# A one-core MoE backbone: the experts' down weights move from the SyncE DMA queue to the ScalarE DMA queue

## What is computed

```python
def moe_ffn(h, router_w, router_bias, w_gate, w_up, w_down, sh_gate, sh_up, sh_down):
    scores = jax.nn.sigmoid(h.astype(jnp.float32) @ router_w.astype(jnp.float32))
    _, idx = lax.top_k(scores + router_bias.astype(jnp.float32), TOP_K)      # 8 of 64 experts
    ...
    def expert_block(args):
        tok, e = args
        xb = h_pad[tok]
        hid = jax.nn.silu(xb @ w_gate[e]) * (xb @ w_up[e])                   # 1024 -> 256
        return hid @ w_down[e]                                               # 256 -> 1024
    ...
```

## Time and profile before

| | us |
|---|---|
| time, median of 3 runs | 2188.66 (2185.78 to 2189.01) |
| the profiled execution, its own time | 2187.06 |
| its span, first to last instruction | 2185.2 |
| PE busy in the span | 1723.6 (79%) |
| ACT busy in the span | 321.0 (15%) |

### The profile page before, as it was taken

How to read it: one execution, slowest core, us unless ns; L and a number is a source line. 1 busy time by engine, 2 the same in 40 slices (tenths; PEclk the granted TensorE clock), 3 DMA queues, 4 the chain that set the end, 5 groups by cost and what they waited for, 6 DMA issues and landing times. The chain is left out here.

```text
span 2185.2 us, 23250 instructions
## 1 busy us (share of the span) xinstructions
PE 1723.6 (79%) x8645; PEld 784.1 (36%) x8645; DVE 590.6 (27%) x1343; ACT 321.0 (15%) x698; POOL 252.3 (12%) x235
## 2 busy tenths in 40 slices
PE   4999999985999899989966997876967657547740
PEld 2544444452443333333323444442422212212210
DVE  2213445252222122222116426431211111101106
ACT  2002333020111111111101105310100000000000
POOL 0301222000111111111100002101111100100002
PEclk8999999997999999999987998887988878778975
DMA  9325662044699999999948140062789999999944
GB/s 339 109 77 184 215 232 102 0 185 183 231 419 421 412 402 386 416 415 397 415 178 342 77 154 5 0 240 95 270 331 382 367 388 367 365 375 371 387 159 173
DMA packets 130368, 577.27 MB, mean 264 GB/s; under 512 B 20146, under 2 KB 25665, under 8 KB 79824
## 3 DMA queue, kind: packets, MB, share of 16 engines
q1 hardware_dynamic: 108112, 523.75, 60.8%
q0 software_dynamic: 22144, 52.02, 6.4%
HBM read 559.91 MB, written 43.05 MB: 276 GB/s over the span
## 5 line engine op out<-in xcount | busy, mean ns | idle before, releaser
L1600 PE MATMUL ps<-wb,pool 128*32 128x512 f32 (+2 forms) x3168 | 570.1, 649 | 200.1 <-issue 198.5
L1600 PEld LDWEIGHTS ps<-wb,pool 128*32 128x32 f32 (+2 forms) x3168 | 188.6, 132 | 577.0 <-issue 577.0
L1614 DVE TENSOR_TENSOR moe_hid<-moe_sg,ps 128x256 f32<-128x256 f32 x74 | 31.1, 421 | 838.4 <-ACT moe_sg L1608 838.4
L1640 PE MATMUL ps<-hT,moe_hidT 128*32 128x512 f32 (+2 forms) x808 | 203.9, 595 | 9.9 <-DVE moe_hidT L1629 7.6
L1640 PE MATMUL ps<-pool,moe_hidT 128*32 128x512 f32 (+2 forms) x776 | 203.6, 595 | 7.7 <-DVE moe_hidT L1629 5.5
L1525 POOL DMA_INDIRECT y_rows<-moe_y,moe_index x74 | 74.2, 1003 | 1048.6 <-ACT moe_y L1656 1027.1
L2005 PE MATMUL ps<-wb,hT 128*128 128x512 f32 x320 | 140.3, 600 | 1.6 <-issue 1.6
L1608 ACT ACTIVATE moe_sg<-ps 128x256 f32<-128x256 f32 x74 | 28.4, 384 | 716.1 <-PE ps L1600 716.1
L1574 PE MATMUL ps<-const,pool 128*128 128x128 f32 x592 | 97.6, 289 | 21.3 <-DMA pool<-h_rows,moe_index 21.3
L1517 POOL DMA_INDIRECT pool<-h_rows,moe_index x74 | 75.2, 1016 | 293.9 <-DVE moe_index L1564 272.0
L1574 PEld LDWEIGHTS ps<-const,pool 128*128 128x128 f32 x592 | 80.2, 195 | 63.1 <-issue 41.6
(11 more groups left out here) (288 smaller groups left out, 1639.7 us busy)
## 6 DMA issues: line engine op xcount, KB each, us to landing
wb<-in_expert_w_gate_dram SPq DMA_DIRECT2D x128, 1024.0 KB, 10.7
wb<-in_expert_w_up_dram SPq DMA_DIRECT2D x128, 1024.0 KB, 16.1
pool<-in_expert_w_down_dram SPq DMA_DIRECT2D x64, 1024.0 KB, 15.4
hT<-in_expert_w_down_dram SPq DMA_DIRECT2D x64, 1024.0 KB, 14.5
wb<-in_ada_w_dram SPq DMA_DIRECT2D x24, 2048.0 KB, 9.6
mix_yr<-y_rows SPq DMA_DIRECT2D x8, 2048.0 KB, 10.6
wb<-in_diff_w_in_dram SPq DMA_DIRECT2D x6, 2048.0 KB, 14.8
wb<-in_ab_w_in_dram SPq DMA_DIRECT2D x4, 2048.0 KB, 16.4
```

Source lines behind the costliest of these rows:

```text
L1600: mm = nc.tensor.matmul(core.ps[lo:lo + width, n % 2, :], xT[:, n % 2, k, lo:lo + width], w[:, k], start=k == 0, stop=k == KD - 1, skip_gr ...
L1640: mm = nc.tensor.matmul(core.ps[lo:lo + width, 2 + half, :], hidT[:, n % 2, k, lo:lo + width], wd_at(q % RING, half, k), start=k == 0, sto ...
```

## The change

`sp_weights` is split. `sp_gate_up` on SP has the gate and up transfers alone, from expert 4 on. `act_down` on ACT has the down transfers: those of experts 0 to 3 ahead of ACT's first instruction of the stage, the others behind `act_y` of the round that frees their slot. Nothing else differs: the same transfers, slots, sizes and semaphores.

```diff
-        def sp_weights(sp, q):
+        def sp_gate_up(sp, q):
+            sp.wait_ge(gu_ready, plan.last(q - RING) + 1)
+            r.load_gate_up(sp, q, r.expert(sp, q))
+
+        def act_down(act, q):
+
             s = q % RING
-            e = r.plan.seq[q] if q < plan.static else r.expert(sp, q)
+            e = r.plan.seq[q] if q < plan.static else r.expert(act, q)
             if q >= RING:
-                sp.wait_ge(gu_ready, plan.last(q - RING) + 1)
-                r.load_gate_up(sp, q, e)
-                sp.wait_ge(down1_ready, plan.last(q - RING) + 1)
+                act.wait_ge(down1_ready, plan.last(q - RING) + 1)
             src = r.of(r.down_src, e)
             if s < 2:
-                sp.dma_start(wd[:, s, :], src).then_inc(d_in[s], 16)
+                act.dma_start(wd[:, s, :], src).then_inc(d_in[s], 16)
             else:
-                sp.dma_start(core.hT[:, 4 * (s - 2):4 * (s - 1), :].rearrange("p k t -> p (k t)"), src).then_inc(d_in[s], 16)
+                act.dma_start(core.hT[:, 4 * (s - 2):4 * (s - 1), :].rearrange("p k t -> p (k t)"), src).then_inc(d_in[s], 16)
...
-                for q in range(E):
-                    sp_weights(sp, q)
+                for q in range(RING, E):
+                    sp_gate_up(sp, q)
...
             def _(act):
+                for q in range(RING):
+                    act_down(act, q)
                 act_take_x(act, 0)
                 for n in range(R):
                     if n >= 1:
                         act_y(act, n - 1)
+                        for q in range(RING, E):
+                            if plan.last(q - RING) == n - 1:
+                                act_down(act, q)
                     act_silu(act, n)
```

## The result

The changed kernel takes 2212.51 us in the median of 4 runs (2209.16 to 2217.46), the kernel before 2187.91: a ratio of 1.0115, 95% interval [1.0094, 1.0136]. It is slower by 24.6 us, where I had forecast slower by 60. The sign and the range (2170 to 2265) held. Ratios leave out one execution of a later kernel (the first run of one queue), which took 2905 us at a granted clock of 0.59 where the others have about 0.9; the median given there, 2155.80, would be 2155.66 without it.

A forecast was written before the change was run, and what follows sets the result against it. Layer 1 from round 7 on was taken as bound by DMA bytes, PE waiting for gate and up weights. Terms 15.0 + 37.1 + 4.5 + 3 = 59.6 us on 2187.06 gave 2247 us, range 2170 to 2265.

The forecast's parts named there:

- Removed: SP's wait for `down1_ready` goes, so the second expert's gate issues earlier; worth nothing because the pipe was full.
- What bounds it: Layer 1 from round 7 on is a race for bytes: PE waits for gate and up weights, not downs.
- the unit: Time per 1 MB transfer with busy DMA engines in layer 1, taken as 3.0 us from three waits.
- rival 1: Service in issue order: S (gate/up products' start) at T (previous end) + 15.6; 15 us gained, 2172; 0.23 together with rival 4.
- Equal turns: SP's and ACT's queues each get half the DMA engines while both have work; 0.60 for 2220 to 2265.
- seven trios behind smaller rounds: Layer 1 waits of three-expert rounds behind one- or two-expert rounds: pipe empty 5.3 us more each, 37.1 us.
- six behind a trio: Layer 1 waits of three-expert rounds right behind another: downs take half rate from gate and up, +2.5 us each, 15.0.
- ACT's cost of zero: ACT's added number reads and down issues, 3.3 to 5.3 us, are covered before silu; cost 0.
- Rival 3: ACT blocks on its queue, issues take over 3 us and silu is late; 2287 us, chance 0.05.
- Layer 0: The pipe can't empty there; gate and up come later by about one down, once: +3 us.
- six short waits: Layer 1 waits under 3 us, for gate and up issued at T; number read behind SP's wait adds 0.75 us each, 4.5.
- The rule: Several issuing engines share the 16 DMA engines; read as time, about no change, 2187: rival 2, chance 0.10.

The follow-up runs named there:

- one-queue kernel: Against the kernel before: all transfers stay on SP's queue, issued as gate and up of all freed slots at T, then their downs; 2155.80, again 2155.19 us.
- the read ahead: Changed kernel (two queues) with the expert's number read ahead of SP's wait for the slot; 2204.23, again 2204.10 us, ratio 1.0083.
- half-size runs: Half of each down matrix fetched, in the kernel with one queue and in that with two and the number read ahead; 2077.16 and 2103.83 us.

## Why the prediction was right, and where it was wrong

| term | forecast, us | measured, us |
|---|---|---|
| SP's wait for the downs removed, new order of issue ("Removed") | 0 | -31 (2155.2 against 2186.5) |
| downs on a queue of their own | +55 (15 + 37 + 3) | +49 (2204.1 against 2155.2) |
| number read behind the wait | +4.5 | +8.8 (2212.9 against 2204.1) |
| sum | +60 | +26 in those runs, +24.6 in the first ones |

**What bounds it** was right: layer 1 from round 7 on, gate and up and not down.

**The wrong step** is in "Removed": "But the pipe was full in that time, so an earlier issue alone gives nothing." That term was put at 0 and measured -31 us. It rested on one number for the unit, 3.0 us, fitted to three waits, pauses and POOL's transfers included; with a number fitted to them the waits could only come out as full pipes. From 1600 to 2050 us the profile lists 151 issues of expert weights in the kernel before and 161 and 162 in the two runs of the one-queue kernel: 2.98 us a transfer before, 2.8 with the new order. At 2.8 us each, the 10 or 11 transfers more make about 30 us. The pause could be seen. In the trace before, this is the time to landing of the down of 32, issued at 1816.18:

```profile
L1507 SPq DMA_DIRECT2D pool<-in_expert_w_down_dram x1: 333/333/333, 1816.2 to 1816.2; - x1
...
DMA to landing us min/median/max: 4.9/4.9/4.9
```

4.9 us is what a transfer takes with nothing ahead of it (5.1). So the queue had no backlog left when SP at last issued it, and from 1816 to 1818 us the engines moved 307 GB/s, where they moved 434 in the two us before. The DMA share of 0.93 said the same, and I explained it away. With the new order a trio behind a trio has one down fewer ahead of it and no such pause. That is rival 1's gain, which I had capped at 35 us and guessed at 15; its S at T + 15.6 for round 17 measured T + 16.0 and T + 14.5 in the one-queue kernel.

**Equal turns** was right, as the landings show in pairs. The term of +55 measured +49, but its parts were not all right, and the closeness of the sum is in part luck. The seven trios behind smaller rounds were forecast at +37 and measured +40 and +41, and the reason that I gave is seen: the pipe stands empty ahead of T. The six behind a trio were forecast at +15 and measured +0.2 and +1.9. For those I had four units start at T + 3.6 and only 2.1 of them landed when the downs join; in the changed kernel three had landed 10.5 us behind T of 16 (the third at 1840.3), before the first down. The pause ahead of T may help here too, since no backlog is left in front of them (share 0.00 against 0.92 above); that was not tested by itself. Against the kernel before, where a part of the 31 us gained is mixed in, these six went -1.6 us each and the seven +4.1.

**ACT's cost of zero** held. ACT issues in 0.34 us, and the wait of silu is still one for PE's products (`L1611` after `L1603`, 745.4 us in 74 times, where it was 716.1). Rival 3 was no case.

**Layer 0** was forecast at +3; alone, with the read behind the wait, it measured +3.6 (1.0019), an interval of 1 to 7 us.

**The read** was put at six short waits, +4.5, and nothing for the thirteen long ones. It cost 8.8. The long waits start later as well: with the read ahead, the six stretches up to a trio behind a trio are 2.7 to 5.9 us shorter than in the changed kernel and the seven others 1.7 to 2.6. What layer 0 has of it was not separated.

**The rule** of the Trainium skill (DMA: Bandwidth & Descriptors, section "Issuing engines are not separate DMA queues") holds as to where the bytes go: both queues run on the same 16 engines and interleave, as the paired landings show, and two queues move no more than one (404 GB/s in layer 0, where one moved 409). Read as "a second queue changes no time" it does not hold in this kernel, where the interleaving cost 49 us of 2155.

One thing is open. The half-size runs leave some 27 us of cost on half the bytes, slightly more than half of 49. Whether a small part of the cost is due to the 0.6 us later issue behind `act_y` was not tested.

## What to carry to other kernels

A queue is also an order. When the DMA engines are the bound, put transfers that are needed later *behind* the others in the same queue; on a queue of their own they take equal turns and overtake. Before calling a pipe full, look for transfers that land in the unloaded time in the middle of it, and don't fit the unit to the waits that it is to explain. Price a change of issue order and a change of queue as two terms, since here they were -31 and +49. Read what an issue needs from a table ahead of the wait and not behind it; here that was worth 8.8 us.

## What the runs showed of the hardware

Two hardware queues with work take turns so evenly that their 1 MB transfers land within 0.8 us of one another (1846.0 and 1846.7, 1852.1 and 1852.9), one of each in 5 to 6 us, where two transfers of one queue with nothing else under way land 2.5 us apart (1815.5 and 1818.0). The two queues together move as much for each unit of busy share as one (410 and 409 GB/s). ACT issues a transfer in 0.34 us, as fast as SP (0.33 to 0.38). With three of four slots in use, what the ring fetched ahead of need is missing as work for the engines later, which showed as a DMA share of 0.89 against 0.97 for the same order of issue, and of 0.00 against 0.92 just ahead of T of 16.
